# Weight sums of a Strassen feed-forward layer: from GpSimd to VectorE, with later transposes at both ends

## The reference

```python
x = layer_norm(DN_ALPHA * x + mixed, ln1_g[i], ln1_b[i])        # mixed = ... @ w_out
h = jnp.square(jax.nn.relu(x @ w_up[i])) @ w_down[i]            # 1024 -> 4096 -> 1024
x = layer_norm(DN_ALPHA * x + h, ln2_g[i], ln2_b[i])
ple = (p[i] @ w_ple[i]) * jax.nn.sigmoid(x @ w_ple_gate[i])     # p is 1024 x 256
x = layer_norm(DN_ALPHA * x + ple, ln3_g[i], ln3_b[i])
```

## Time and profile before

| | us |
|---|---|
| median of 3 runs | 4180.81 (4176.88 to 4183.77) |
| profiled execution, device time | 4178.59 |
| its span, first to last instruction | 4176.9 |
| feed-forward layer in it, first to last product | 3306.8 to 3993.3 |
| mean granted TensorE clock | 0.974 |

### The profile page before, as it was taken

The page is one execution under the profiler, slowest core; times in us unless marked ns, Lnnn a source line. Parts: engine busy times, 40 slices in busy tenths (PEclk is TensorE's granted clock), DMA queues, the critical chain, the costliest instruction groups (busy, mean ns, idle before and its releaser), DMA issues.

```text
span 4176.9 us, 58913 instructions
## 1 busy us (share of the span) xinstructions
PE 3902.3 (93%) x25804; PEld 3141.5 (75%) x25804; DVE 2052.3 (49%) x2740; ACT 1496.9 (36%) x2361; POOL 1174.6 (28%) x577
## 2 busy tenths in 40 slices
PE   8899999999999999999999889999999889999987
PEld 4757576765998997676687777897888777777767
DVE  2545464533340248762205463332186577868754
ACT  3232323222332144562213353222275254453543
POOL 1202020102124356661232102342102622232234
PEclk9999999999999999999999999999999999999989
DMA  3101010003101121000111000221101122212111
GB/s 91 32 2 32 2 32 2 17 11 117 41 31 51 41 81 41 27 29 31 36 46 51 31 1 23 66 97 31 41 1 40 52 72 73 67 52 65 47 51 41
DMA packets 165743, 177.03 MB, mean 42 GB/s; under 512 B 8944, under 2 KB 136816, under 8 KB 165488
## 3 DMA queue, kind: packets, MB, share of 16 engines
q1 hardware_dynamic: 165488, 173.28, 13.2%
HBM read 164.87 MB, written 8.39 MB: 41 GB/s over the span
## 4 chain that ended last, share of the span: by engine, by line
PE 75%; DVE 12%; ACT 6%; POOL 4%; issue 3%; DMA 0%; POOLq 0%; SPq 0%; DVEq 0%; ACTq 0%
PE pair L722 10%; PE pair L724 10%; PE pair L723 10%; PE pair L687 9%; PE pair L1473 4%; PE pair L1475 4%; PE pair L1476 4%; PE pair L710 3%; DVE W_r L3355 2%; PE pair L698 2%; PE pair L1218 1%; PE pair L1408 1%; PE pair L677 1%; PE pair L872 1%; POOL H L3702 1%
## 5 line engine op out<-in xcount | busy, mean ns | idle before, releaser
L3642 POOL TENSOR_TENSOR W_r<-W,W_r 128x2048 fp32r<-128x2048 f32 (+1 forms) x74 | 326.6, 4414 | 743.8 <-ACT W_r L1583 743.8
L722 PE MATMUL pair<-XT_r,W_r 128*128 128x512 f32 x1232 | 495.2, 402 | 6.3 <-ACT BIG L2130 1.9
L724 PE MATMUL pair<-XT_r,W_r 128*128 128x512 f32 x1232 | 480.9, 390 | 0.0
L723 PE MATMUL pair<-BIG_r,W_r 128*128 128x512 f32 x1112 | 434.0, 390 | 0.0
L687 PE MATMUL pair<-XT,W 128*128 128x512 f32 x928 | 405.5, 596 | 3.2 <-POOL MIX L3515 2.2
L1473 PE MATMUL pair<-W_r 128*128 128x512 f32 x896 | 358.0, 400 | 46.3 <-DVE W_r L3355 40.6
L1475 PE MATMUL pair<-W_r 128*128 128x512 f32 x896 | 355.5, 397 | 0.0
L1476 PE MATMUL pair<-W_r 128*128 128x512 f32 x896 | 355.3, 396 | 0.0
L687 PEld LDWEIGHTS pair<-XT,W 128*128 128x128 f32 x928 | 175.1, 191 | 220.1 <-issue 218.6
L722 PEld LDWEIGHTS pair<-XT_r,W_r 128*128 128x128 f32 x1232 | 232.1, 188 | 63.0 <-issue 10.0
L724 PE MATMUL pair<-W_r,MIX_r 128*128 128x256 f32 x960 | 271.6, 283 | 0.0
(11 more groups left out here) (465 smaller groups left out, 8616.3 us busy)
## 6 DMA issues: line engine op xcount, KB each, us to landing
W<-w_in SPq DMA_DIRECT2D x29, 1024.0 KB, 5.4
W<-w_in_e SPq DMA_DIRECT2D x33, 512.0 KB, 6.5
W<-w_in_o SPq DMA_DIRECT2D x12, 1024.0 KB, 5.1
BIG<-w_up SPq DMA_DIRECT2D x20, 512.0 KB, 3.6
MIX<-w_up SPq DMA_DIRECT2D x20, 512.0 KB, 3.6
MIX<-w_down SPq DMA_DIRECT2D x20, 512.0 KB, 3.6
BIG<-w_down SPq DMA_DIRECT2D x20, 512.0 KB, 3.6
W<-w_in SPq DMA_DIRECT2D x17, 512.0 KB, 4.1
```

What stands on the lines that cost most here:

```text
L722: E.matmul(b[:, 0:n], lh, rh, start=k == ks[0], stop=False)
L723: E.matmul(b[:, 0:n], lh, rl, start=False, stop=False)
L724: mm = E.matmul(b[:, 0:n], ll, rh, start=False, stop=k == ks[-1])
L3642: G.tensor_tensor(WLO[k % 2][:, 0:n], WSTAGE[k % 2][:, 0:n], WHI[k % 2][:, 0:n], ALU.subtract).then_inc(*s_split.mark("split", k))
```

## The change

- The weight sums leave GpSimd's queue (`pool_mlp` is gone) and stand in VectorE's: six of unit 0 at the end of `dve_outp`, the others in `dve_mlp` at fixed places between low parts. The sums keep their operands and buffers.
- In the output product before the layer, each tile's two last products are separate steps and the transposes' lag is 7 in place of 3; the filler matmuls before the transposes of tiles 6 and 7 are gone.
- The table's transposes move into product 2, behind its third quarter, and their copies with them.
- After the layer tiles 4 to 7 are transposed after 11 steps, in one row; GpSimd normalises tiles 5 and 7 too; the low part of the gate weights' second quarter goes from GpSimd to VectorE.
- The gate products of the first two column quarters are done for tiles 0 to 3 first and then for tiles 4 to 7; eight of them (were four) stand before the end of the layer's stage.

```diff
-                        ("outp", {6: 5, 7: 14}), ("mlp", {0: 7})):
+                        ("mlp", {0: 7})):
...
-        LN_DVE = (5, 7)
+        LATE = 11
         def copy_lag(st, t):
-            return 3 if st is not outp else 1 if t < 4 else 2
+            if st is outp:
+                return 1 if t < 4 else 2
+            return LATE - 1 if st is ff and t >= 4 else 3
...
-        G_ORDER = [(q, t) for q in range(2) for t in range(NT)] + [(q, t) for t in range(NT) for q in (2, 3)]
-        G_EARLY = 4
+        G_ORDER = [(q, t) for half in range(2) for q in range(2) for t in range(4 * half, 4 * half + 4)] + [(q, t) for t in range(NT) for q in (2, 3)]
+        G_EARLY = 8
...
         def pe_ln_tile(st, lag=1):
-                yield from nothing(lag)
+                yield from nothing(LATE if st is ff and t >= 4 else lag)
...
                 for t in range(NT):
                     pe_out3(2, t)
+                    yield None
                     pe_out3(3, t)
                     yield t
-                yield None
+                for _ in range(3):
+                    yield None
                 for c in range(4):
                     pe_part(0, c)
                     if c % 2:
                         yield None
+                        yield None
-            follow(steps(), pe_ln_tile(outp, 3))
+            follow(steps(), pe_ln_tile(outp, 7))
...
                     for c in range(4):
                         pe_part(g, c)
+                        if g == 2 and c == 2:
+                            pe_table()
...
-                    if j == 3:
-                        for at in G_ORDER[0:2]:
-                            pe_gate_product(*at)
                     yield 4 + j
-                for at in G_ORDER[2:G_EARLY]:
+                for at in G_ORDER[0:G_EARLY]:
                     pe_gate_product(*at)
                     yield None
...
                     dve_low(1, k, "x")
                     yield None
+                for k in range(2):
+                    for p in (5, 7, 6):
+                        dve_w_sum(0, p, k)
...
+        def dve_w_sum(u, p, k):
+            for role in (0, 2, 3):
+                dve.wait_ge(*done("mlp", "raw", u, role, k))
+            dve.wait_ge(*ff.dve.last())
+            V.tensor_tensor(*w_sum(u, p, k)).then_inc(*ff.dve.mark("mlp", "w_sum", u, p, k))
...
-                    if not is_up(u) and p == 2:
-                        dve_sum(u, 6, 1)
+                    if not is_up(u) and p == 1:
+                        dve_w_sum(u, 5, 1)
+                        dve_w_sum(u, 7, 0)
                     if g < LAST_P:
                         dve_low(g + 1, 0, "w")
                         dve_low(g + 1, 0, "x")
...
                     if is_up(u):
+                        if p == 1 and u:
+                            for other in (5, 7, 6):
+                                dve_w_sum(u, other, 1)
...
+                        if p == 5:
+                            for k in range(2):
+                                dve_w_sum(u, 3, k)
...
+                        if p == 4:
+                            dve_w_sum(u + 1, 5, 0)
-                    elif p == 1:
-                        for other, k in ((5, 0), (6, 0), (5, 1)):
-                            dve_sum(u, other, k)
+                    else:
+                        if p == 1:
+                            dve_sum(u, 5, 0)
+                            dve_w_sum(u, 6, 0)
+                            dve_sum(u, 6, 0)
+                        if p == 2:
+                            dve_w_sum(u, 7, 1)
+                            dve_w_sum(u, 6, 1)
+                            dve_sum(u, 5, 1)
+                            dve_sum(u, 6, 1)
+                        if p in (6, 5):
+                            for k in range(2):
+                                dve_sum(u, 7 if p == 6 else 3, k)
+                            dve_w_sum(u, 4, 0 if p == 6 else 1)
+                        if p in (7, 3) and u + 1 < UNITS:
+                            for k in range(2):
+                                dve_sum(u + 1, 5 if p == 7 else 6, k)
+                        if p == 4 and u + 1 < UNITS:
+                            for other in (5, 7, 6):
+                                dve_w_sum(u + 1, other, 0)
                     if g < LAST_P:
                         dve_low(g + 1, 1, "w")
                         dve_low(g + 1, 1, "x")
...
                 for t in range(4, NT):
                     yield t
+                dve.wait_ge(*done("gate", "high", 1))
+                V.tensor_tensor(WL[1][:, :], STAGE[1], WH[1][:, :], ALU.subtract).then_inc(*gate.dve.mark("gate", "split", 1))
...
-            pool_mlp()
             pool_low(gate, 0)
             pool_ln(ff)
-            pool_low(gate, 1)
```

More of the change, by code:

```diff
@@ L1483, in pe_part, with pe_table @@
                 ff.pe.note("mlp", "used", g, k)
+        def pe_table():
+            pe.wait_ge(*done("mlp", "read", 1, 1))
+            for c in range(2):
+                for hf in range(2):
+                    pe_transposes(gate, for_ln, ("p_tr", c, hf),
+                                  [PN[:, hf * 4 + i, c * P:(c + 1) * P] for i in range(4)], done("gate", "pn"))
         def pe_mlp():
@@ L2412, in steps @@
                         act_squared_relu(g - 1, k)
+                        if g == 2 and k == 0:
+                            for c in range(2):
+                                act_copy_out(gate, for_ln, ("p_tr", c, 0), PTT[:, c, 0:HALF], HALF)
+                            gate.act.note("gate", "ptt_act")
                 for t in range(4):
@@ L2421, in steps @@
                         act_split_high(gate, 1, done("gate", "staged", 1), done("mlp", "used", LAST_P, 0))
-                    if j == 3:
-                        for k in range(2):
-                            act_gate_root(k)
                     yield 4 + j
-                for k in range(2, G_EARLY):
+                for k in range(G_EARLY):
                     act_gate_root(k)
@@ L2613, in tile @@
                                        ALU.mult).then_inc(*st.dve.mark(st.name, "shift", t))
-                if st is ff and t in LN_DVE:
-                    yield
-                    dve.wait_ge(*done("rows", "mlp"))
-                    dve.wait_ge(*done("mlp", "unit", t))
-                    V.tensor_tensor(H[:, t, :], H[:, t, :], ROWS[:, 0:D], ALU.mult).then_inc(*st.dve.mark())
-                    dve.wait_ge(*st.dve.last())
-                    V.tensor_tensor(H[:, t, :], H[:, t, :], ROWS[:, D:2 * D], ALU.add).then_inc(
-                        *st.dve.mark("mlp", "ln", t))
-                    yield from nothing(2)
-                else:
-                    yield from nothing(copy_lag(st, t))
+                yield from nothing(copy_lag(st, t))
                 if not split:
@@ L3399, in steps @@
                     u, p = product_of(g)
-                    if g == 3:
-                        for c in range(2):
-                            dve_copy_out(gate, for_ln, ("p_tr", c, 1), PTT[:, c, HALF:SEQ], HALF)
-                        gate.dve.note("gate", "ptt_dve")
                     for k in range(2):
@@ L3414, in steps @@
                         dve_low(g + 1, 0, "x")
+                    if g == 2:
+                        for c in range(2):
+                            dve_copy_out(gate, for_ln, ("p_tr", c, 1), PTT[:, c, HALF:SEQ], HALF)
+                        gate.dve.note("gate", "ptt_dve")
                     if is_up(u):
+                        if p == 1 and u:
+                            for other in (5, 7, 6):
+                                dve_w_sum(u, other, 1)
                         if u == 0 and p == 2:
@@ L3683, in pool_ln @@
             for t in range(NT):
-                if st is ff and t in LN_DVE:
-                    continue
                 x = H[:, t, :]
@@ L3826, in pool_sum @@
                          {5: (r0, r2, r0), 7: (r2, r3, r2), 6: (r3, r3, r0), 4: (r1, r1, r3)})[p]
-            for role in (0, 2, 3):
-                pool.wait_ge(*done("mlp", "raw", u, role, k))
-            if is_up(u) and p == 6 or not is_up(u) and p == 5:
-                pool.wait_ge(*done("mlp", "lw", number(u, 1), k))
-            if p in (3, 4):
-                pool.wait_ge(*done("mlp", "lw", number(u, 2), k))
-            pool.wait_ge(*ff.pool.last())
-            G.tensor_tensor(dst, x, y, ALU.add if is_up(u) and p == 5 else ALU.subtract).then_inc(
-                *ff.pool.mark("mlp", "w_sum", u, p, k))
-        def pool_mlp():
-            for u in range(UNITS):
-                for k in range(2):
-                    for p in (5, 7, 6):
-                        pool_sum(u, p, k)
-                for k in range(2):
-                    pool_sum(u, 3 if is_up(u) else 4, k)
+            return dst, x, y, ALU.add if is_up(u) and p == 5 else ALU.subtract
         def gpsimd_program():
@@ L4136, in sp_gate @@
                 if quarter == 1:
```

(3 more changed lines are left out.)

18 lines of the change are left out of this document (1 added, 17 removed).

## The result

The changed kernel takes 4112.65 us (median of 4 runs, 4109.79 to 4121.68), beside 4178.85 us of the kernel before (4 runs, 4175.11 to 4183.77): ratio 0.9845, 95% interval 0.9826 to 0.9863. That is 66 us faster; 4109 was predicted.

The account below looks back on a forecast made before the run. TensorE, busy 93% of the span, was taken as the bound, losing time to waits (VectorE slowed by GpSimd's sums) and lower clock. 4178.6 - 43.5 - 7.7 - 21.1 = 4106.3, plus 2.2 for the median: 4109 us, range 4095 to 4132.

Parts of the forecast that it names:

- Sums on VectorE: Feed-forward units from product three: weight sums on VectorE leave 12.8 us of stalls in place of 56.3, -43.5 us.
- The layout: VectorE's new order worked out from a down unit's first product: TensorE stalls 3.2 us per down unit.
- The spacings of rows 5: VectorE, earlier trace: 1.26 and 1.33 us when waiting for the operation before, 1.14 otherwise; the skill says semaphores cost nothing extra.
- The start: Before product three of the layer: it starts at 3352.3 in place of 3360.05, -7.7 us.
- the fillers' removal gains 2 us: Start: without filler matmuls ahead of the last two transposes, product one starts near 3323.6, was 3325.6.
- The end: From 4023.1 on: TensorE ends at 4133.1 in place of 4154.2, -21.1 us.
- the sum of 104.7 + 0.8 + 4.2 + 0.3: End: TensorE's work, tile 3's low-part wait, the fourth weight quarter's wait and latencies, in us, added to 4023.1.
- No gain at the end: Rival, end: tiles 6 and 7 wait for gate products, 6 us gained for 21, 4124; chance 0.13.
- Clock in the down units: Rival: remaining pauses in down units lower the clock, +14 us, 4123, or 4131 with later low parts; chance 0.13.
- GpSimd isn't what holds TensorE: Rival, layer: ScalarE's eight operations hold TensorE, so the time stays, 4181; chance 0.03.
- Sums hidden wholly: Rival, layer: the added sums on VectorE cost no stalls, 4109 - 12.8 = 4096; chance 0.07.
- VectorE the bound: Rival, every unit: sums of 3.3 us make VectorE the bound, slower, 4270; chance 0.04.

Follow-up runs that it names:

- the idle subtractions: Changed kernel plus GpSimd subtractions (128 x 896) on unused memory that nobody waits for: 4161.68 us, ratio 0.9954 to the kernel before.
- the memsets: Kernel with the idle subtractions, each replaced by three GpSimd memsets of the same 896 columns: product three to the layer's end 589.67 us.
- the reads without that wait: Changed kernel, down-unit reads waiting for VectorE's last but one operation instead of its last: product three to the layer's end 587.39 us.
- kernel without the stage's wait: Changed kernel without TensorE's wait for the feed-forward stage's end ahead of the remaining gate products: 162.30 us behind the layer.
- one sum later: Changed kernel with product 7's second-half weight sum moved behind the next two low parts in down units: product three to the layer's end 589.67 us.
- kernel with the sums alone: Kernel before with the sums on VectorE and the table's transposes in product two, start and end as before: 4129.85 us, ratio 0.9871.

## Why the prediction was right, and where not

*Sums on VectorE* (43.5 predicted, 43.8 measured). Right in cause and size. The layout gave stalls of 0.9, 0.6, 1.5, 0.1 and 0.1 us per down unit; the products take 11.70, 11.66, 12.29, 11.00 and 10.98, so 0.82, 0.78, 1.41, 0.12 and 0.10. All borders are undisturbed, and from product three on no low part or sum is over 1.3 us. That GpSimd's sums stretch VectorE's operations had been inferred from the earlier trace rows; the idle subtractions and the memsets show it, and that it is GpSimd's reading. The spacings of rows 5 against the rule of the Trainium skill: the trace was right, since the reads without that wait follow closer.

*The start* (7.7 predicted, 7.5 measured) was right in its total and wrong inside, and that the total fits is luck. Product zero came at 3308.2, product one at 3322.2, not 3323.6. The two waits came as laid out: 2.0 us inside product one for VectorE's last copy, which was done at 3325.6, not 3326.8, and 2.6 us (2.9 predicted) ahead of product two, which VectorE's sums set. All of that chain, product two's start with it, was 1.2 us sooner than laid out. Against it stands the half-speed stretch behind the second wait (0.88 over 14.34 us, 1.7 us), which the forecast had only in its bounds: the two errors cancel. That the fillers' removal gains 2 us was wrong: beside GpSimd's sums the start's edits bring 2.3, beside VectorE's they lose 1.1: 0.7 by the tile order and 0.4 by the fillers, whose removal brings product two 1.2 us sooner and then costs 1.6 of clock.

*The end* (21.1 predicted, 16.9 measured) is the step that was mis-sized. The mechanism held: eight gate products in a row, the four late tiles' transposes back to back (32 in 3.66 us from 4007.63), no wait for tiles 5 to 7, 22.65 us behind TensorE's last matmul. Two terms were missing from the sum of 104.7 + 0.8 + 4.2 + 0.3. The first is the wait for the end of the stage that stands in the code ahead of the remaining gate products: with the transposes late, VectorE's eight subtractions of four tiles are the stage's end, 2.6 us after TensorE was ready. The second is the clock behind waits, 1.5 us behind this one and 1.5 behind the split's. Without the stage's wait the end takes 162.3, which is 183.4 - 21.1, but the clock loss behind the split's wait is still in that figure, so the sum itself was about 1.5 too high. Most of it is the transposes: priced at 1.09 us a tile, 5.4 for five, which is the recorded duration with its latency. From start to the next start tile 3's take 0.79 (3982.73 to 3983.52, changed kernel) and the four late tiles' 3.41 (kernel without the stage's wait), 4.2 in all:

```profile
4003.51 3.65 PE L712 MATMUL pair<-ident,H 128*128 128x128 f32 x32
4006.92 0.36 PE L724 MATMUL pair<-W_r,XT_r 128*128 128x256 f32 x1
```

VectorE's split of the second quarter, priced at 2.3 us, took 4.23 beside a GpSimd operation that took 4.31 in place of 2.4. It cost nothing: tile 7 was normalised 51.7 us behind the layer, 52.1 in the forecast. The fourth quarter's, with GpSimd idle, took 2.29 on VectorE.

How much of the end's gain one execution shows is in part chance: the same code behind the layer took 163.6 to 166.8 us in eight traces, by the lower clock alone or nearly so, and the changed kernel's 166.52 is near the upper end.

*The rivals.* No gain at the end: refuted, tiles 5 to 7 are not waited for. Clock in the down units: 1.00. GpSimd isn't what holds TensorE: refuted, with GpSimd's sums gone the middle falls by 43.8 us, and idle subtractions alone bring 40 back. Sums hidden wholly: the weight sums cost 3.3 us, but 9.3 of the 12.8 were there without any of them, by the layout from ScalarE and the activation sums; so that rival had the wrong split of what remains. VectorE the bound: only within 1.4 us of a down unit's middle (one sum later moves the stall, it doesn't remove it).

## What to carry to other kernels

Before asking how much work an engine has, look at what stretches its operations: if one operation has two durations (1.22 and 2.6 to 3.4 us here), find what runs beside the long ones, and count moving that work onto the stretched engine as a gain. When work is moved past a wait for "the end of a stage", read what the end now is. And idle matmuls that bridge a wait are not worth their own length when they are taken away: here the fillers took 1.27 and 3.29 us (kernel with the sums alone), their removal brought 1.2, since a wait for VectorE took their place, and the lower clock behind cost 1.6.

## What the runs showed of the hardware

- In code that is the same, the kernels here came between 7.0 us sooner and 11.3 later than the kernel before at the same matmul, 3254 us into the program. That is of the size of the spread of one kernel's runs (4174.6 to 4188.97 for the kernel before, nine runs). The changed kernel's 11.3 arise in the first 1000 us, whose granted clock is 0.96 where that of the kernel before has 0.97:

```profile
0.00:1000.00 1000.00, 916.81 (x9022) 637.22 (x9023) 461.79 (x820) 302.80 (x608) 137.59 (x156) 0.96 0.11 33
```

- Each stretch at the lower clock cost 1.5 to 1.8 us, and the length of a wait alone doesn't tell whether one follows. At the start it followed waits of 2.0 and 2.6 us, and neither one of 2.4 alone nor two of 2.0 and 2.1. Behind the wait of 2.6 us for the stage's end it came in all nine traces that have it; behind the split's wait of 2.2 us, the same code each time, in four of twelve (0.97 and 1.00 above). Why is open.
- GpSimd memsets beside VectorE cost nothing (143.9 us of them), GpSimd subtractions (141.2 us of them) 40 us in the same places.
